# A transformer trunk on one core: the first norm's roots applied behind the in-projection, and the MLP's last part by seven chained products

## The reference

```
def rms_norm(x, g):
    return x * rsqrt(mean(x * x, -1) + EPS) * g

xn = rms_norm(h, norm_mix)
proj = xn @ w_in                       # to fox q, k, v and gate, conv (mLSTM q, k), mLSTM v, o, i, f, and two branch gates
... forgetting attention, mLSTM, merge, mix; cross-attention ...
hn = rms_norm(h, norm_mlp)
a = relu(hn @ w_mlp_in)                # 1024 -> 4096
h = h + (a * a) @ w_mlp_out            # 4096 -> 1024
return rms_norm(h, norm_final)
```

## Time and profile before

| | us |
|---|---|
| Median of 3 runs | 935.72 (935.67 to 935.85) |
| The profiled execution | 935.99 |
| its span, first to last instruction | 934.3 |
| TensorE busy in it | 921.0 |
| VectorE busy | 551.6 |
| ScalarE busy | 427.6 |

### The profile page before, as it was taken

One profiled execution on the slowest core, in us unless ns is written; L12 is line 12 of the kernel. 1 busy time (PEld: TensorE's weight loads), 2 busy tenths in 40 slices (PEclk: granted clock), 3 DMA queues, 4 the chain that ended last, 5 costly groups with the idle time before them and its releaser, 6 DMA issues.

```text
span 934.3 us, 11910 instructions
## 1 busy us (share of the span) xinstructions
PE 921.0 (99%) x4614; PEld 758.3 (81%) x4614; DVE 551.6 (59%) x997; ACT 427.6 (46%) x744; POOL 15.5 (2%) x40
## 2 busy tenths in 40 slices
PE   7999999999999999999999999999999999999997
PEld 6878778777787888889888778988888888888886
DVE  5534777424557645778143545668847956885543
ACT  5544466534433314345244543376346436534523
POOL 5000000000000000000000000000000000000000
PEclk9999999999999999999999999999999999999999
DMA  7311222122201552344421432120621261062202
...
DMA packets 44687, 92.10 MB, mean 99 GB/s; under 512 B 1764, under 2 KB 1864, under 8 KB 44632
## 3 DMA queue, kind: packets, MB, share of 16 engines
...
q10 hardware_dynamic: 16, 0.00, 0.0%
...
## 4 chain that ended last, share of the span: by engine, by line
PE 87%; DVE 7%; ACT 4%; issue 1%; ACTq 0%; POOL 0%; DVEq 0%; POOLq 0%
PE bank L1504 64%; PE bank L1535 12%; DVE w_lo L1093 2%; DVE conv_acc L1180 2%; PE bank L1660 1%; PE bank L1709 1%; ACT w_hi L795 1%; PE bank L1548 1%; PE bank L1646 1%; PE bank L1687 1%; PE bank L1674 1%; DVE peak L1367 1%; PE bank L1602 1%; PE bank L1629 1%; PE bank L1614 0%
## 5 line engine op out<-in xcount | busy, mean ns | idle before, releaser
L1504 PE MATMUL bank<-act_hi,w_hi 128*128 128x512 f32 (+1 forms) x640 | 247.7, 387 | 0.1
L1504 PE MATMUL bank<-act_hi,w_lo 128*128 128x512 f32 (+1 forms) x640 | 242.8, 379 | 0.0
L1504 PE MATMUL bank<-act_lo,w_hi 128*128 128x512 f32 (+1 forms) x640 | 242.4, 379 | 0.0
L1089 DVE TENSOR_TENSOR w_lo<-stage,w_hi 128x1024 fp32r<-128x1024 f32 x130 | 153.0, 1220 | 65.0 <-ACT w_hi L795 64.6
L795 ACT ACTIVATE w_hi<-stage 128x1024 fp32r<-128x1024 f32 x130 | 130.3, 1051 | 89.7 <-PE bank L1504 31.7
L1504 PEld LDWEIGHTS bank<-act_hi,w_lo 128*128 128x128 f32 x640 | 120.3, 188 | 23.1
L1504 PEld LDWEIGHTS bank<-act_hi,w_hi 128*128 128x128 f32 x640 | 120.6, 188 | 22.2 <-DVE w_lo L1089 0.6
L1504 PEld LDWEIGHTS bank<-act_lo,w_hi 128*128 128x128 f32 x640 | 120.6, 188 | 21.3
L1504 PE MATMUL bank<-w_hi,act_hi 128*128 128x512 f32 (+1 forms) x264 | 102.9, 390 | 3.8 <-DVE act_lo L1321 2.0
L1504 PE MATMUL bank<-w_hi,act_lo 128*128 128x512 f32 (+1 forms) x264 | 101.2, 383 | 0.0
L1504 PE MATMUL bank<-w_lo,act_hi 128*128 128x512 f32 (+1 forms) x264 | 101.1, 383 | 0.0
...
## 6 DMA issues: line engine op xcount, KB each, us to landing
stage<-in_w_in SPq DMA_DIRECT2D x20, 1024.0 KB, 5.0
stage<-in_w_mlp_in SPq DMA_DIRECT2D x16, 1024.0 KB, 5.3
stage<-in_w_mlp_out SPq DMA_DIRECT2D x16, 1024.0 KB, 5.5
stage<-in_w_xkv SPq DMA_DIRECT2D x8, 1024.0 KB, 4.9
stage<-in_w_mix_out SPq DMA_DIRECT2D x4, 1024.0 KB, 4.9
stage<-in_w_xq SPq DMA_DIRECT2D x4, 1024.0 KB, 5.7
stage<-in_w_xo SPq DMA_DIRECT2D x4, 1024.0 KB, 4.9
...
```

The lines of the kernel that those rows point to most:

```text
L1089: dve.tensor_tensor(w_lo[:, r:r + 2, :], stage_pair(pair), w_hi[:, r:r + 2, :].bitcast(F32), ALU.subtract).then_inc(s_low, 1)
L1504: ins = pe.matmul(dst, still[q], moving[q], start=(k == 0 and q == 0), stop=(k == nk - 1 and q == 2))
```

## The change

Two things at once.

**Roots behind the projection.** x goes unscaled into the transposes and the in-projection, and `norm_turn` for the first four tiles waits for x alone. The roots are computed beside this into `x_root`. For projections with tokens in rows (fox_v, ml_v) the root is the scale of ScalarE's copy. For those with tokens in columns it is needed as a row: a new step `spread_roots`, ahead of half 9, has VectorE scale the identity by the roots of each tile (four diagonals), TensorE multiply them by ones into bank 7, and ScalarE copy this to `row_root`. VectorE then takes each such group out of PSUM with a multiplication by the row, and ScalarE's part (high copy, tanh, conv tap) follows from SBUF. GpSimd copies the row to `row_root_late` for the gates. The order of the first steps is new, the warm-up is (6, 1), and conv's steps come one half later.

**Chained products.** Round 3 becomes an `mlp_out` unit like the others. In all four rounds products now run on in the same PSUM banks by CHAIN (product 2 adds onto 0, 3 onto 1, 4 onto 2, 6 onto 4), and each fold adds the sum so far into a quarter of `h_tok`, so that the partial results and `combine` are gone. A product that goes on in a bank waits for the fold of what is in it. There is a fourth stage buffer for the fourth lot. In round 3 the order of the last products is q5 and q6 for m = 0, q5 for m = 1, and q6 for m = 1 in two parts of 256 columns. The final norm goes by tiles 0, 2, 1, 3 and begins with the right half of the columns, and GpSimd applies the gain to that half.

```diff
-WARM_UP = (6, 9)
+WARM_UP = (6, 1)
 
 
 LAST = FF // DM - 1
 PRODUCTS = 7
+SUM_OF = ((0, 0), (1, 1), (0, 1), (0, 1), (1, 1), (0, 0), (1, 0))
+CHAIN = (0, 1, 0, 1, 0, 2, 0)
+READ_BEFORE = {2: 0, 3: 1, 4: 2, 6: 4}
+ADDED_BEFORE = {3: 2, 4: 1, 5: 0, 0: 5, 1: 4, 2: 3, 6: 6}
+LAST_TILES = (0, 2, 1, 3)
...
-        if r < LAST:
-            u.append((f"mlp_out{r}", "w_mlp_out", r * DM, 4 * PRODUCTS, 0, 2))
-    u += [
-        ("mlp_last0", "w_mlp_out", LAST * DM, KT, 0, NT),
-        ("mlp_last1", "w_mlp_out", LAST * DM, KT, HALF_W, NT),
-    ]
+        u.append((f"mlp_out{r}", "w_mlp_out", r * DM, 4 * PRODUCTS, 0, 2))
...
+            halves += [(n, m, q, 0, HALF_W) for q in cs[:-2] for m in groups]
+            halves += [(n, 0, q, 0, HALF_W) for q in cs[-2:]] + [(n, 1, cs[-2], 0, HALF_W)]
+            halves += [(n, 1, cs[-1], lo, hi) for lo, hi in ((0, EDGE), (EDGE, HALF_W))]
...
-            for (h, half), buf in zip(((0, 0), (0, 1), (1, 1), (1, 0)), (a, b, c, c)):
+            for (h, half), buf in zip(((0, 0), (0, 1), (1, 1), (1, 0)), (a, b, c, STAGES)):
...
-    steps += [("norm", 0), ("split_weights", 0), ("norm_turn", 0), ("norm_split", 0), ("split_weights", 1),
-              ("split_weights", 2), ("norm", 1), ("split_weights", 3), ("norm_root", 1), ("norm_scale", 1)]
-    after(1, ("norm_turn", 1), ("norm_split", 1), ("norm", 2))
-    after(2, ("norm_turn", 2), ("norm_split", 2), ("norm", 3))
-    after(4, ("norm_turn", 3), ("norm_split", 3), ("split_weights", 4), ("split_weights", 5))
+    steps += [("norm_turn", 0), ("norm_split", 0), ("split_weights", 0), ("split_weights", 1)]
+    before(1, ("norm_turn", 1), ("norm_split", 1), ("split_weights", 2), ("split_weights", 3), ("norm", 0),
+           ("norm_root", 0))
+    before(3, ("norm_turn", 2), ("norm_split", 2), ("norm", 1), ("norm_root", 1))
+    before(5, ("norm_turn", 3), ("norm_split", 3), ("norm", 2), ("norm_root", 2))
+    after(5, ("norm", 3), ("norm_root", 3), ("split_weights", 4), ("split_weights", 5))
+    before(first("fox_q") + 1, ("spread_roots", 0))
+    for p in range(2 * PAIRS):
+        after(group_end(UNIT["fox_q" if p < PAIRS else "fox_k"], p % PAIRS), ("fox_low", p))
...
-        after(g + 1, ("conv_tanh", c))
-        after(g + 2, ("conv_silu", c))
+        after(g + 1, ("conv_sum", c))
+        after(g + 2, ("conv_tanh", c))
+        after(g + 3, ("conv_silu", c))
...
-    for t in range(8):
-        after(first(f"mlp_in{2 * LAST}") + 2 + t, ("combine", t))
-    n = UNIT["mlp_last1"]
-    for i in range(NT):
-        after(group_end(n - 1, i) - 1, ("norm_first", 3 * NT + 2 + i))
-        after(group_end(n, i) - 1, ("norm", 3 * NT + 2 + i))
-    for v in range(4 * LAST):
+    n = UNIT[f"mlp_out{LAST}"]
+    t0 = 3 * NT + 2
+    for i, (m, q) in enumerate(((1, 3), (1, 4), (1, 4), (1, 4))):
+        after(HALF_AT[(n, m, q)], ("norm_first", t0 + i))
+    for i, (m, q) in enumerate(((0, 5), (0, 6))):
+        after(HALF_AT[(n, m, q)], ("norm", t0 + i), ("norm_root", t0 + i), ("norm_scale", t0 + i))
+    after(len(HALVES) - 3, ("norm", t0 + 2))
+    after(len(HALVES) - 2, ("norm_root", t0 + 2), ("norm_second", t0 + 3))
+    after(len(HALVES) - 1, ("norm_scale", t0 + 2), ("norm", t0 + 3), ("norm_root", t0 + 3), ("norm_scale", t0 + 3))
+    for v in range(4 * (LAST + 1)):
...
-        if step == "norm" and n != 1:
+        if step == "norm" and NT <= n < 3 * NT + 2:
...
+        stage.append(at(f"stage{STAGES}", 72, [P, LOT, HALF_W]))
...
+                elif buf == STAGES:
+                    sp.wait_ge(s_nturn, 2 * n_norm)
...
+            pool.wait_ge(s_row_root, 1)
+            pool.wait_ge(s_fturn, N_FOX)
+            pool.tensor_copy(row_root_late[:], row_root[:]).then_inc(s_row_late, 1)
...
+            for i in range(NT):
+                n, tile = n_norm + i, LAST_TILES[i]
+                row, s_row, loads = norm_gains(n)
+                pool.wait_ge(s_row, 16 * loads)
+                pool.wait_ge(s_fold, folds(LAST, 3 + tile // 2, tile % 2))
+                pool.wait_ge(s_first_sum, n - NT - 1)
+                c = norm_columns(n)[0]
+                first = norm_source(n)[:, c]
+                pool.tensor_tensor(first, first, row[:, c], ALU.mult).then_inc(s_weighed, 1)
...
                 if k == "fox_q":
-                    act.activation(fq_hi[:, j, :], b[:], ACT.Copy, scale=FOX_HD ** -0.5).then_inc(s_qhigh, 1)
+                    taken(act, g)
+                    copy(fq_hi[:, j, :], fq_scaled[:, j, :]).then_inc(s_qhigh, 1)
                 elif k == "fox_k":
-                    copy(fk_hi[:, j, :], b[:]).then_inc(s_qhigh, 1)
+                    taken(act, g)
+                    copy(fk_hi[:, j, :], fk_scaled[:, j, :]).then_inc(s_qhigh, 1)
                 elif k == "fox_v":
-                    copy(fox_v[:, j, :], b[:]).then_inc(free, 1)
+                    act.wait_ge(s_xroot, j + 1)
+                    copy(fox_v[:, j, :], b[:], scale=x_root[:, j:j + 1]).then_inc(free, 1)
...
                 elif k in ("gate_fox", "gate_ml"):
                     t = 4 * order(n) + j
                     dst = gate_f[:, t, :] if k == "gate_fox" else gate_m[:, j, :]
-                    if k == "gate_ml" and order(n) == 1:
-                        act.wait_ge(s_merged, 4)
-                    if k == "gate_ml" and order(n) == 0:
-                        act.wait_ge(s_silu, 2 * 4)
+                    taken(act, g)
                     col = t + (KT if k == "gate_ml" else 0)
                     act.wait_ge(s_prep, 1)
-                    act.activation(dst, b[:], ACT.Tanh, scale=0.5, bias=gate_bias[:, col:col + 1]).then_inc(free, 1)
+                    act.activation(dst, dst, ACT.Tanh, scale=0.5, bias=gate_bias[:, col:col + 1]).then_inc(s_tgate, 1)
...
+                elif step == "spread_roots":
+                    act.wait_ge(s_spread, 1)
+                    copy(row_root[:], bank[7][:]).then_inc(s_row_root, 1)
...
-                dst = (p1, p5, p6, quarter(0, 1), p7, quarter(0, 0), quarter(1, 0))[q][:, m, :]
-                src = two[1 + (PRODUCTS * r + q) % 3][:, m, :]
-                if r > 0:
-                    dve.wait_ge(s_fold, folds(r - 1, q, m))
-                elif q in (3, 5, 6):
-                    taken(dve, GROUP0[UNIT[f"x_out{int(q == 3)}"]] + (2 + m if q == 6 else m))
+                low, c = SUM_OF[q]
+                dst, src = quarter(low, c)[:, m, :], two[1 + CHAIN[q]][:, m, :]
+                before = ADDED_BEFORE[q]
+                if before < q:
+                    dve.wait_ge(s_fold, folds(r, before, m))
+                elif r > 0:
+                    dve.wait_ge(s_fold, folds(r - 1, before, m))
+                else:
+                    taken(dve, GROUP0[UNIT[f"x_out{c}"]] + 2 * low + m)
                 dve.wait_ge(s_half, i + 1)
-                if r == 0 and q in (0, 1, 2, 4):
-                    dve.tensor_copy(dst, src).then_inc(s_fold, 1)
-                else:
-                    dve.tensor_tensor(dst, src, dst, ALU.add).then_inc(s_fold, 1)
-
-            def combine(t):
-
-                dst, more = ((quarter(0, 0), p1), (p6[:], p1), (quarter(0, 1), p6), (quarter(0, 1), p5), (p7[:], p6),
-                             (quarter(1, 1), p7), (quarter(1, 0), p7), (quarter(1, 1), p5))[t]
-                if t == 0:
-                    dve.wait_ge(s_fold, folds(LAST - 1, 6, 1))
-                else:
-                    dve.wait_ge(s_combined, t)
-                dve.tensor_tensor(dst, dst, more[:], ALU.add).then_inc(s_combined, 1)
+                if i == len(HALVES) - 2:
+                    dve.tensor_tensor(dst[:, 0:EDGE], src[:, 0:EDGE], dst[:, 0:EDGE], ALU.add).then_inc(s_edge, 1)
+                    return
+                if i == len(HALVES) - 1:
+                    dve.wait_ge(s_edge_sum, 1)
+                    dst, src = dst[:, EDGE:HALF_W], bank[0][:, EDGE:HALF_W]
+                dve.tensor_tensor(dst, src, dst, ALU.add).then_inc(s_fold, 1)
+                if r == LAST and (q, m) == (4, 1):
+                    dve.wait_ge(s_fold, folds(LAST - 1, 6, m))
+                    dst = quarter(1, 0)[:, m, EDGE:HALF_W]
+                    dve.tensor_tensor(dst, src[:, EDGE:HALF_W], dst, ALU.add).then_inc(s_edge_sum, 1)
...
                 if k == "fox_q":
-                    dve.wait_ge(s_qhigh, j + 1)
-                    dve.scalar_tensor_tensor(fq_lo[:, j, :], b[:], FOX_HD ** -0.5, fq_hi[:, j, :].bitcast(F32),
-                                             ALU.mult, ALU.subtract).then_inc(free, 1)
+                    group_done(dve, g)
+                    dve.wait_ge(s_row_root, 1)
+                    dve.scalar_tensor_tensor(fq_scaled[:, j, :], b[:], FOX_HD ** -0.5, row_root[:],
+                                             ALU.mult, ALU.mult).then_inc(free, 1)
                 elif k == "fox_k":
-                    dve.wait_ge(s_qhigh, PAIRS + j + 1)
-                    dve.tensor_tensor(fk_lo[:, j, :], b[:], fk_hi[:, j, :].bitcast(F32), ALU.subtract)\
```

(42 more changed lines are left out.)

209 lines of the change are left out of this document (110 added, 99 removed).

## The result

The changed kernel takes **950.97 us** (median of four runs, 949.56 to 951.53), the kernel before 935.79 beside it: a ratio of 1.0159 (95% interval 1.0146 to 1.0171), 15.2 us slower. The prediction said 939.7, with a range that ended at 944.5. Its sign was right and its size was not: it had about a quarter of the loss. The profiled execution took 951.47 us and spans 949.2, 14.9 more than before; I account for those 14.9.

The account below looks back on a forecast made before the run. TensorE, busy 921.0 of 934.3 us, was taken to bound the kernel. Terms -5.6 + 0.1 + 5.8 + 0.6 + 2.6 + 0.5 = +4.0 us on the median 935.72 gave 939.7 us, range 933.0 to 944.5.

Parts of the forecast that it names:

- MLP, -5.6: Last part of the MLP: seven chained products for two groups save 5.6 us of TensorE's path, with no fold stopping it.
- rival D: MLP: a fold over 8.2 us late stops TensorE, 1 us in each of four rounds, 943.7 us; chance under 0.05.
- First tiles, +0.1: Start: half 0 ends a microsecond early, half 1 waits for weights behind tile 1, half 2 starts at 19.7; +0.1 us.
- rival A: Start: TensorE's clock drops after new pauses, half 0 costs some +1.9 us; 941.6, up to 944.5 us; chance 0.20.
- Root row, +5.8: Ahead of half 9: TensorE waits for VectorE's diagonals, queued behind late splits of pairs 8 and 9; +5.8 us.
- Rival B: Before half 9: the weight block of pairs 8 and 9 is not late, +3.1 us instead of 5.8, 937.0 us; chance 0.20.
- VectorE's new work, +0.6 and +2.6: Multiplications by the root row on VectorE: +0.6 us in the projections, +2.6 us in the mLSTM attention.
- End, +0.5: Tail: last matmul's start to last scaling grows from 2.42 to 2.9 us, VectorE's queue being late by q5's fold; +0.5 us.
- Rival C: Whole kernel: VectorE stays ahead at the root row and in attention, so only TensorE's work counts; 931.6 us; chance 0.15.

Follow-up runs that it names:

- with the pauses filled: The changed kernel with idle products of ones by ones put into TensorE's three long pauses, no wait moved; 945.00 us.
- the MLP runs: Kernel before with the chained-products half alone, 933.79 us; the same with GpSimd's gain multiplications held back until VectorE has split the last weights, 933.53 us.
- all of it mended: Kernel before plus the chained-products half, with GpSimd's gain multiplications held back, scaling of tiles 0 and 1 behind the next fold, four result buffers; 931.50 us.
- The one with all mends: Changed kernel with diagonals made early, weights 2 and 3 split before tile 1, 14 idle products, and four edits of the end; 932.20 us.

## Why the prediction was right or wrong

**MLP, -5.6: right** (5.56 measured). The count of halves and the slack of the chain held; no fold stopped TensorE, and rival D is out. (The last part before was 216 matmuls, not 192; the 18 halves that the sum goes by are right.)

**First tiles, +0.1: the waits right, the step that failed is the clock.** Without the clock's part the term measures +0.05 (half 2 at 19.68 against 19.63). The pauses were foreseen ("from 6.5 to 9.9, and again from 13.4 to 17.0") and rival A asked what they do to the clock, at a chance of 0.20, with "by the rows alone the warm start is as good". The trace of before has no TensorE pause longer than 1.3 us before the end of its work, so its rows could not speak for a warm start behind one of 3.5 us. A pause that the trace has never shown should have made A at least as likely as the forecast. A's own sign came true, matmuls 0.43 us apart in the first 15 us. A's price was also short. It let half 0 pay 1.9 us where it cost 2.7 (half 1 at 19.51 against 16.82 with the pauses filled), and half 1 perhaps, and did not ask the question of the third pause, which the forecast itself had put before half 9. The three cost 7.6 us between the profiled executions, 6.0 between the medians.

**Root row, +5.8: right where the clock is full** (6.05 from half 2 to half 9 with the pauses filled). In the changed kernel the same stretch gave 6.7, as the products of the row ran at half clock, and half 9 at half clock gave 1.9 more. Each link was there: DMA late by its buffer, the splits of pairs 8 and 9, the diagonals. Rival B is out.

**VectorE's new work, +0.6 and +2.6: right** (+0.9 and +2.7), the second by the means named, the gates. What makes up the 0.9 wasn't tried.

**End, +0.5: wrong, +3.1.** Two steps failed. The durations were taken from the trace of before, where GpSimd does nothing at the end; beside it VectorE's splits take 3.45 us in place of 2.35, twice, and the first fold of the four comes 1.8 us late by it (916.28 against 914.46 in the MLP runs). And the sum allowed for one late fold, q5's, but not for a row of tiles that is late from its first. Each tile's norm is about 3.24 us long on VectorE, in order, against 2.72 us between TensorE's sums, so a late first tile stays late, and more so. A third thing had not been read at all, the wait for the result's buffer; it did not hold in the changed kernel, but was next in line. With all of it mended the end is 7.0 us long, 0.7 more than before, which is near the +0.5.

**Rival C** (931.6, all waits hidden) was not this kernel. The one with all mends comes near it, 932.20, but by luck: C has +0.1 at the start and nothing in the attention, where that kernel has about -3.1 and +3.6.

In sum, of the 10.9 us between the forecast's +4.0 and the trace's +14.9, 7.6 are the clock, 2.6 the end, and the rest lies in small terms. The clock alone, priced at 7.6 on the three pauses that the forecast had in it, would have made the forecast 947.3, still 3.7 under the median; with the end as well, 949.9.
